# Linear attention in a two-block decoder: state steps issued as one batch, its exponentials moved into the levels, the output product begun on six split tiles

## The chip, the cores and the metric

One Trainium2 chip, of which the kernel uses a single core. Work is done by TensorE (PE in the rows, with its weight load as PEld), VectorE (DVE), ScalarE (ACT) and GpSimd (POOL); SyncE (SP) issues the loads. The metric is the time of the whole kernel on the device in microseconds (us), as a median of runs; a profile is one execution more, taken by the hardware profiler. The granted clock of TensorE is given as a share of 2.4 GHz: 1.00 is that, 0.50 is 1.2 GHz.

## What is computed

Two stacks of two layers on 256 tokens of width 1024, all in float32. The change lies in the first stack, whose layers mix tokens in three ways (a short convolution, an attention with sinks, a gated linear attention) and join them in one product with `w_out`. The first layer works on 512 columns (256 tokens of x, 256 of the context), the second on 256. The part in question, per direction (0 forward, 1 backward) and head:

```python
def step(state, inp):                       # gla_chunk_scan
    b = jnp.cumsum(gc.astype(jnp.float32), axis=2)
    b_last = b[:, :, -1:, :]
    new_state = (jnp.exp(b_last[:, :, 0, :])[..., None] * state
                 + jnp.einsum('bhsk,bhsv->bhkv', kc * jnp.exp(b_last - b), vc))
    ...
    o = (jnp.einsum('bhts,bhsv->bhtv', a, vc)
         + jnp.einsum('bhtk,bhkv->bhtv', qc * jnp.exp(b), state))
    return new_state, o

def gla_output(o, g, norm_g):
    o32 = o32 * lax.rsqrt(jnp.mean(o32 * o32, axis=-1, keepdims=True) + EPS) * norm_g.astype(jnp.float32)
    ...
    return (o32.reshape(B, T, GLA_HEADS * GLA_DV) * jax.nn.silu(g.astype(jnp.float32))).astype(g.dtype)
...
x = x + gt1 * (jnp.concatenate([conv_x, attn_x, gla_x], axis=-1) @ w_out)
```

## The kernel before

Activations lie feature-major: 128 channels of a tile on the partitions, tokens along the free dimension, eight tiles for a width of 1024. Weights come as pieces of 1 MB through `ring`, six slots that SP fills as TensorE frees them. Each large product is made of three in a reduced float format: ScalarE rounds a piece to `ring_hi` (line 220), VectorE takes the remainder `ring_lo` (line 223), and the moving side is split the same way (`a_hi`, and `mix_lo` or `h_lo`). `split_ahead` does this some pieces ahead of TensorE, and `pe_products` runs four output groups side by side over the eight tiles of the input, then the others.

Every engine runs its own program in the order written; engines meet at semaphores, and at `phase_end`, where PE, ACT and DVE wait for one another. In a layer of the first stack the order is: products with `w_in` (`b1_groups`), rope and convolution, attention, gates (`pe_gla_gates`), levels, state steps (`..._gla_out`), head norm (`..._gla_norm`), output product, feed-forward.

**Levels.** The products inside a tile of 128 tokens are built in seven levels. In each, DVE multiplies keys and queries with exponentials (`scaled`, lines 1114 and 1115), takes the differences for the next level (`decay`, lines 1105 and 1106), and copies the masked grams of this level from PSUM (line 1136); ACT takes the exponentials (line 1085); PE makes the grams. Into the six first levels TensorE puts two products of the modulation each (`pe_mod_piece`; ACT copies their rows at line 810). When all levels are done it turns all rows into columns (`pe_mod_columns`) and DVE takes them (`dve_mod_take`).

**State steps.** With four tiles of tokens and two directions there are six steps. For each: ACT takes two exponentials into the single buffer gX (line 1198), DVE multiplies the keys (line 1217), PE turns them (line 1171), ACT copies them (line 1202), PE multiplies them with the values, DVE adds the result to the decayed state (line 1226), and PE uses the state on the next tile's queries. One buffer of each kind serves all steps. The products of grams and values follow.

**Head norm.** ACT copies the sums from PSUM (line 1254), squares them, and for each half of the channels takes a logarithm (line 1260) and an exponential (line 1261) of the head means that PE makes, then Silu of the gate (line 1263). DVE multiplies (lines 1270, 1274). Then the eight tiles of `mixT` are split (lines 473 and 478), then three pieces of `w_out`, then the product starts.

## Time and profile before

| | us |
|---|---|
| median of 3 runs | 2932.71 (2929.97 to 2933.93) |
| the profiled execution, its own time | 2932.67 |
| its span, first to last instruction | 2930.9 |
| TensorE busy | 2595.3 (89%) |
| VectorE busy | 1824.8 (62%) |
| ScalarE busy | 1494.5 (51%) |
| DMA | 561.57 MB, mean 192 GB/s |

The shares are means over stages with different limits. The stages of the change are found by the lines named above in the timeline, once per layer of the first stack: around 288 to 414 us and around 1039 to 1136 us. The rest of the program is not touched in what it does. A row of a timeline gives start, length, engine, line, operation, what is written and read, and in brackets how long the engine had been idle and what ended that. A float32 product counts as two records of TensorE.

### The profile page before, as it was taken

What the parts mean: (1) busy time and instruction counts of PE and PEld (TensorE: products, weight loads), DVE (VectorE), ACT (ScalarE), POOL (GpSimd) and SP (SyncE); (2) the same over time, 40 slices, a digit from 0 to 9 for tenths busy, and PEclk for the clock granted to TensorE, in tenths of its full rate; (3) what the DMA queues carried; (4) which work ended last, traced back from release to release, by engine and by line L of the source; (5) the groups of instructions that cost most, each with busy time, mean ns of one, the idle gap of its engine ahead of it and who ended that gap; (6) DMA issues with size and microseconds to landing.
All of it is one profiled execution on the core that took longest, in us unless ns stands there. A gap on an engine that the chain in (4) does not pass through costs nothing.

```text
span 2930.9 us, 42838 instructions
## 1 busy us (share of the span) xinstructions
PE 2595.3 (89%) x17130; PEld 2294.3 (78%) x17130; DVE 1824.8 (62%) x2532; ACT 1494.5 (51%) x1936; POOL 10.6 (0%) x53
## 2 busy tenths in 40 slices
PE   5987559999999766999878999968799999999997
PEld 3865448999999555998858999948788888888886
DVE  2245736545543554555845554856698889888986
ACT  3225344434442334444455443455577777777775
POOL 0000000000000000000000000000000000000000
PEclk8998869999998866999969999979999999999998
DMA  6241403555532341453404454403299899899994
GB/s 258 99 189 44 173 7 142 182 178 181 187 137 108 115 173 58 173 187 141 162 1 144 144 185 175 159 29 130 85 352 356 337 374 351 338 357 351 354 357 190
DMA packets 80205, 561.57 MB, mean 192 GB/s; under 512 B 8705, under 2 KB 12033, under 8 KB 12434
## 3 DMA queue, kind: packets, MB, share of 16 engines
q1 hardware_dynamic: 79746, 557.86, 51.2%
q8 instruction: 138, 2.26, 0.3%
q0 software_dynamic: 272, 1.05, 0.1%
q14 instruction: 49, 0.40, 0.1%
HBM read 557.82 MB, written 1.05 MB: 191 GB/s over the span
## 4 chain that ended last, share of the span: by engine, by line
PE 52%; DVE 6%; ACT 4%; issue 1%; ACTq 0%; PEldq 0%; DVEq 0%; PEld 0%
PE psum L229 50%; DVE ring_lo L223 2%; DVE Z L1360 1%; ACT ring_hi L220 1%; PE psum L1700 1%; DVE hT L710 1%; PE psum L633 0%; DVE hT L380 0%; ACT L407 0%; DVE xT L313 0%; ACT hT L674 0%; DVE Z L1373 0%; DVE Z L1226 0%; ACTq L183 0%; DVE hT L421 0%
## 5 line engine op out<-in xcount | busy, mean ns | idle before, releaser
L223 DVE TENSOR_TENSOR ring_lo<-ring,ring_hi 128x2048 fp32r<-128x2048 f32 x479 | 1096.5, 2291 | 460.9 <-ACT ring_hi L220 457.9
L220 ACT ACTIVATE ring_hi<-ring 128x2048 fp32r<-128x2048 f32 x479 | 915.9, 1914 | 391.0 <-PE psum L229 389.7
L229 PE MATMUL psum<-a_hi,ring_hi 128*128 128x256 f32 (+1 forms) x2448 | 733.1, 299 | 99.3 <-DVE ring_lo L223 57.4
L229 PE MATMUL psum<-a_hi,ring_lo 128*128 128x256 f32 (+1 forms) x2448 | 729.3, 298 | 0.0
L229 PE MATMUL psum<-h_lo,ring_hi 128*128 128x256 f32 (+1 forms) x2128 | 630.9, 296 | 0.0
L229 PEld LDWEIGHTS psum<-a_hi,ring_hi 128*128 128x128 f32 x2448 | 478.9, 196 | 116.9 <-issue 84.7
L229 PE MATMUL psum<-ring_hi,a_hi 128*128 128x512 f32 (+2 forms) x1744 | 542.5, 377 | 5.9 <-DVE h_lo L429 3.7
L229 PEld LDWEIGHTS psum<-a_hi,ring_lo 128*128 128x128 f32 x2448 | 478.5, 195 | 10.3
L229 PEld LDWEIGHTS psum<-h_lo,ring_hi 128*128 128x128 f32 x2128 | 416.4, 196 | 7.4
L229 PEld LDWEIGHTS psum<-ring_hi,a_hi 128*128 128x128 f32 x1744 | 329.9, 192 | 58.3 <-issue 4.1
L229 PE MATMUL psum<-ring_lo,a_hi 128*128 128x512 f32 (+2 forms) x1040 | 375.1, 361 | 0.0
L229 PE MATMUL psum<-Zr,ring_hi 128*128 128x256 f32 x1408 | 257.3, 286 | 8.1 <-DVE xT L578 8.1
L229 PEld LDWEIGHTS psum<-Zr,ring_hi 128*128 128x128 f32 x1408 | 222.0, 194 | 8.9 <-DVE xT L578 8.9
L229 PEld LDWEIGHTS psum<-ring_lo,a_hi 128*128 128x128 f32 x1040 | 202.0, 194 | 28.2
L229 PE MATMUL psum<-ring_hi,Zr 128*128 128x512 f32 x704 | 219.8, 393 | 0.2
L229 PE MATMUL psum<-Z 64*128 64x128 f32 (+4 forms) x792 | 136.6, 406 | 90.8 <-DVEq L183 28.9
L229 PE MATMUL psum<-Zr,ring_lo 128*128 128x256 f32 x704 | 200.6, 285 | 0.0
L229 PEld LDWEIGHTS psum<-Z 64*128 64x128 f32 (+1 forms) x792 | 86.8, 221 | 124.0 <-issue 36.4
L539 ACT ACTIVATE mixT<-psum 128x256 f32<-128x256 f32 x88 | 33.7, 383 | 262.7 <-PE psum L229 262.7
L229 PEld LDWEIGHTS psum<-ring_hi,Zr 128*128 128x128 f32 x704 | 130.1, 188 | 27.7 <-DVE ring_lo L223 1.8
L229 PE MATMUL psum<-ring_lo,Zr 128*128 128x512 f32 x352 | 137.3, 390 | 0.0
L229 PEld LDWEIGHTS psum<-Zr,ring_lo 128*128 128x128 f32 x704 | 136.5, 194 | 0.0
(249 smaller groups left out, 2515.9 us busy)
## 6 DMA issues: line engine op xcount, KB each, us to landing
ring<-in_stream SPq DMA_DIRECT2D x527, 1024.0 KB, 4.8
cst<-in_constants SPq DMA_DIRECT2D x1, 1216.0 KB
xT<-in_xT SPq DMA_DIRECT2D x1, 1024.0 KB, 9.5
xT<-in_ctxT SPq DMA_DIRECT2D x1, 1024.0 KB, 11.8
xT<-in_memT POOLq DMA_DIRECT2D x1, 1024.0 KB, 6.0
out_y<-hT SPq DMA_DIRECT2D x1, 1024.0 KB, 4.8
Z<-in_level_masks SPq DMA_DIRECT2D x1, 448.0 KB
vec<-in_vectors SPq DMA_DIRECT2D x1, 225.0 KB, 11.0
```

What stands on the lines that cost most here:

```text
L220: e.activation(hi, raw, ACT.Copy).then_inc(sem("piece_rounded"), 1)
L223: e.tensor_tensor(lo, raw, hi.bitcast(F32), ALU.subtract).then_inc(sem("piece_split"), 1)
L229: ins = pe.matmul(*args, **kw)
L539: act.activation(mixT[:, f % 2, 0:T], bank[2 * (f % 2)][:, 0:T], ACT.Silu)\
L710: ins = dve.tensor_tensor_reduce(s_buf(p, i, e)[:, 0:p["nk"]], src, p["mask"], 1.0, p["init"][e], ALU.add, ALU.max, cols(i, MAX)[:, e:e + 1])
L1360: ins = dve.scalar_tensor_tensor(z2(6 + c), CP[:, c, j:j + T], w, z2(6 + c), ALU.mult, ALU.add)
L1700: ins = pe.transpose(bank[2 + j % 2][:, c * P:(c + 1) * P], hid_tok[j % 2][:, c * P:(c + 1) * P], const("ident"))
```

## The change

- **Exponentials.** Those of the queries (`gQ`, one of 1024 or 512 columns a direction) stand behind levels 3 and 4 of ACT's program, those of the keys (six of 128 columns a direction, into six buffers `gK`) behind levels 4 and 5, and tiles 0 to 5 of `mixT` are rounded behind levels 0 to 2. DVE multiplies the keys in three instructions in the last level, ahead of its masked copies, and the queries behind them.
- **Modulation columns.** Each level turns the rows of the level before, four products at a time; the second layer turns the four pieces of the rope stage ahead of its levels. The rows lie in tiles 6 and 7 of `mixT`.
- **State steps.** All six turns, copies (three, two steps each) and key products are independent of the states, go to PSUM banks 4 to 6 and are issued as a batch with the products of grams and values between them. ACT copies the first state of each direction; DVE makes the other four with full 128x128 tiles. States have six buffers. ACT rounds two pieces of `w_out` ahead of its copies, and DVE takes their remainders between the state steps.
- **Head norm and output product.** ACT reads the sums from PSUM. Both logarithms, then both exponentials. Silu of the gate is taken when the gate leaves PSUM in `b1_groups`. The output product is issued behind the last use of a state, with the head means behind its first tile; tiles 6 and 7 are split last. It uses banks 2, 3, 4 and 7.
- Three phase ends a layer are gone from ACT, DVE and PE (levels, state steps, head norm; none is left between gates and the end of the layer's output product).

```diff
-        def pe_products(pe, groups, ready, who=None, late=None):
+        def pe_products(pe, groups, ready, who=None, late=None, at=range(4), inside=lambda k: None):
...
                     if g == front - 1:
+                        inside(k)
                         await_next(pe, ready)
...
-            g += feature_major([zt(15), zt(16)], 0, n)
+            for out, (terms, rows_, width, _, held) in zip((zt(15), zt(16)), feature_major([None, None], 0, n)):
+                g.append((terms, rows_, width, [("function", out, ACT.Silu)], held))
             g += feature_major([lrT(0), lrT(1)], 0, 2 * T, rows_=16)
             return g
 
+
+        B1_WHO = [("act", "dve")[g % 2] for g in range(22)] + ["dve", "act", "act", "dve", "act"]
...
+        KEY_TILES = ((0, 2, 3), (1, 2, 3))
+        STEPS = ((0, 2), (0, 3), (1, 3), (1, 2), (1, 1), (0, 0))
...
+            if layer:
+                pe_mod_columns(pe, IN_ROPE[1])
...
+                if l and in_level(layer, l - 1):
+                    pe_mod_columns(pe, in_level(layer, l - 1))
                 for m in in_level(layer, l):
                     pe_mod_piece(pe, m)
-            first, end = batch(layer)
-            pe_mod_columns(pe, first, end - first, rows_a)
...
-            phase_end(pe)
+            pe.wait_ge(sem("gram_read"), base(pe, "gram_read"))
...
                 for m in in_level(layer, l - 1) if l else ():
-                    act_mod_rows(act, m, batch(layer)[0], rows_a)
-            for m in in_level(layer, LEVELS - 1):
-                act_mod_rows(act, m, batch(layer)[0], rows_a)
-            phase_end(act)
+                    act_mod_rows(act, m)
+                if l < 3:
+                    if layer and l == 0:
+                        act.wait_ge(sem("mod_columns"), ROPE_COLUMNS)
+                    act_split_mix(act, (2 * l, 2 * l + 1), n)
+                if l in (3, 4):
+                    d = l - 3
+                    act.activation(gQ[:, d, :, 0:n], gB[d][:, :, 0:n], ACT.Exp).then_inc(sem("query_exp"), 1)
+                if l in (4, 5):
+                    d = l - 4
+                    for i, t in enumerate(KEY_TILES[d]):
+                        edge = t * P + (P - 1 if d == 0 else 0)
+                        for c in range(2):
+                            ins = act.activation(gK[:, d, c, i, :], gB[d][:, c, t * P:(t + 1) * P], ACT.Exp, scale=-1.0,
+                                                 bias=gB[d][:, c, edge:edge + 1])
+                    ins.then_inc(sem("key_exp"), 1)
...
+                else:
+                    await_next(dve, "key_exp", 2)
+                    for out, t0, t1 in ((gK[:, 0, :, 1:3, :], 2, 4), (gK[:, 1, :, :, :], 1, 4), (gK[:, 0, :, 0:1, :], 0, 1)):
+                        k = GK[:, :, t0 * P:t1 * P].rearrange("p c (s n) -> p c s n", n=P)
+                        dve.tensor_tensor(out, out, k, ALU.mult).then_inc(sem("keys_decayed"), 1)
...
+            await_next(dve, "query_exp", 2)
+            for d in range(2):
+                dve.tensor_tensor(gQ[:, d, :, 0:n], gQ[:, d, :, 0:n], GQ[:, :, 0:n], ALU.mult)\
+                   .then_inc(sem("queries_decayed"), 1)
...
+        def state(d, i):
+            return 3 * d + i
+
+        def kv(j):
+            return bank[4 + j // 2][:, (j % 2) * 256:(j % 2 + 1) * 256]
...
+            def turn(b):
+                await_next(pe, "keys_decayed")
...
+                for j in (2 * b, 2 * b + 1):
+                    d, t = STEPS[j]
+                    for c in range(2):
+                        ins = pe.transpose(kv(j)[:, c * P:(c + 1) * P], gK[:, d, c, KEY_TILES[d].index(t), :],
+                                           const("ident"))
+                ins.then_inc(sem("keys_turned"), 1)
...
+            def within(ts):
+                for t in ts:
+                    for h in range(4):
+                        mm(pe, gO[(h % 2) * HD:(h % 2 + 1) * HD, h // 2, t, :],
+                           tok[:, t * 384 + P + h * HD:t * 384 + P + (h + 1) * HD], gA[:, t, h, :],
+                           start=t % 2 == 0 and h < 2, stop=False, skip_group_check=True)
...
+            def step(b):
+                await_next(pe, "keys_copied")
+                for j in (2 * b, 2 * b + 1):
+                    t = STEPS[j][1]
+                    for c in range(2):
+                        mm(pe, kv(j)[:, c * P:(c + 1) * P], gKt[:, j, c * P:(c + 1) * P],
+                           tok[:, t * 384 + P + c * P:t * 384 + P + (c + 1) * P], start=True, stop=True,
+                           last_of="state_step" if j % 2 and c == 1 else None)
...
+            turn(0)
+            turn(1)
+            within(outs[0:2])
+            turn(2)
+            step(0)
+            step(1)
+            within(outs[2:])
+            step(2)
+            await_next(pe, "queries_decayed", 2)
+            first = base(pe, "state_first")
+            own = base(pe, "state")
+            uses = [(i, d) for i in range(3) for d in range(2) if ORDER[d][i + 1] in outs]
...
+            for i, d in uses:
+                t = ORDER[d][i + 1]
+                if i == 0:
+                    pe.wait_ge(sem("state_first"), first + d + 1)
+                else:
+                    pe.wait_ge(sem("state"), own + 2 * (i - 1) + d + 1)
+                for c in range(2):
+                    for r in range(2):
+                        rr = slice(r * HD, (r + 1) * HD)
+                        last = (i, d) == uses[-1] and c == 1 and r == 1
+                        mm(pe, gO[rr, c, t, :], gS[rr, state(d, i), c, rr], gQ[rr, d, c, t * P:(t + 1) * P],
+                           start=False, stop=True, skip_group_check=True, last_of="gla_sum" if last else None)
...
+        def act_gla_out(act, layer):
+            split_ahead(act, "act", 0)
+            for b in range(3):
+                await_next(act, "keys_turned")
+                act.activation(gKt[:, 2 * b:2 * b + 2, :].rearrange("p j n -> p (j n)"), bank[4 + b][:, :], ACT.Copy)\
+                   .then_inc(sem("keys_copied"), 1)
...
+                await_next(act, "state_step")
+                act.activation(gS[:, state(d, 0), :, :].rearrange("p c n -> p (c n)"), kv(2 * d), ACT.Copy)\
+                   .then_inc(sem("state_first"), 1)
+            advance(act, "state_step", 1)
...
+            def step(d, i):
+                t = ORDER[d][i]
+                j = STEPS.index((d, t))
+                for c in range(2):
+                    ins = dve.scalar_tensor_tensor(gS[:, state(d, i), c, :], gS[:, state(d, i - 1), c, :],
+                                                   gD[:, d, t, c:c + 1], kv(j)[:, c * P:(c + 1) * P], ALU.mult, ALU.add)
+                link(dve, ins)
+                dve.nop().then_inc(sem("state"), 1)
...
+            dve_split_mix(dve, (0, 1), n)
+            split_ahead(dve, "dve", -1)
             for d in range(2):
...
+                await_next(dve, "state_step")
+                await_next(dve, "state_first")
+                step(d, 1)
+            split_ahead(dve, "dve", 1)
+            await_next(dve, "state_step")
             for d in range(2):
...
+                step(d, 2)
+            dve_split_mix(dve, range(2, 6), n)
...
+            n = 2 * T if layer == 0 else T
+            act.preload_act_table_set("natural_log")
+            await_next(act, "gla_sum")
...
             for c in range(2):
-                act.activation(gSq[:, c, 0:n], o[:, c, :], ACT.Square).then_inc(sem("gla_squared"), 1)
+                act.activation(by_tile(gSq[:, c, :], n), gO[:, c, 0:n // P, :], ACT.Square).then_inc(sem("gla_squared"), 1)
...
             for c in range(2):
                 await_next(act, "gla_mean_square")
-                link(act, act.activation(gR[:, c, 0:n], bank[4 + c][:, 0:n], ACT.Ln, bias=EPS))
+                ins = act.activation(gR[:, c, 0:n], bank[5 + c][:, 0:n], ACT.Ln, bias=EPS)
+            link(act, ins)
+            for c in range(2):
...
+                await_next(act, "gla_normed")
+                act_split_mix(act, (6 + c,), n)
```

TensorE, first layer, from the last level on. In the order views x2 counts like instructions in a row; before, this stands six times in a row (three are shown), followed by the sixteen products within tiles and the two head means:

```order
L1171 MATMUL psum<-cst,Z 128x128 x2
L229 MATMUL psum<-tok,Z 128x128 x2
L229 MATMUL psum<-Z 128x128 x2
L1171 MATMUL psum<-cst,Z 128x128 x2
L229 MATMUL psum<-tok,Z 128x128 x2
L229 MATMUL psum<-Z 128x128 x2
```

and now, once, ending in the first product of the output (`cst,mixT` are the last columns, `cst,Z` turns, `Z,tok` products within tiles, `tok,Z` key products, `hT,Z` uses of the states):

```order
L229 MATMUL psum<-cst,mixT 128x2 x4
L1201 MATMUL psum<-cst,Z 128x128 x8
L229 MATMUL psum<-Z,tok 64x128 x8
L1201 MATMUL psum<-cst,Z 128x128 x4
L229 MATMUL psum<-tok,Z 128x128 x8
L229 MATMUL psum<-Z,tok 64x128 x8
L229 MATMUL psum<-tok,Z 128x128 x4
L229 MATMUL psum<-hT,Z 64x128 x24
L229 MATMUL psum<-a_hi,ring_hi 128x512
```

The turns no longer alternate with key products and uses, and the output product has moved ahead of the head means.

ScalarE, first layer, before: the head norm up to the weight pieces.

```order
L1260 ACT_TABLE_LOAD
L1260 ACTIVATE hT<-psum 128x512
L1261 ACT_TABLE_LOAD
L1261 ACTIVATE hT<-hT 128x512
L1260 ACT_TABLE_LOAD
L1260 ACTIVATE hT<-psum 128x512
L1261 ACT_TABLE_LOAD
L1261 ACTIVATE hT<-hT 128x512
L1263 ACT_TABLE_LOAD
L1263 ACTIVATE hT<-Z 128x512 x2
L473 ACTIVATE a_hi<-mixT 128x512 x8
L220 ACTIVATE ring_hi<-ring 128x2048 x3
```

and now, from the weight pieces on:

```order
L220 ACTIVATE ring_hi<-ring 128x2048 x2
L1252 ACTIVATE Z<-psum 128x512 x3
L1256 ACTIVATE Z<-psum 128x256 x2
L1301 ACT_TABLE_LOAD
L1304 ACTIVATE hT<-psum 128x512 x2
L1307 ACTIVATE hT<-psum 128x512 x2
L1310 ACT_TABLE_LOAD
L1310 ACTIVATE hT<-hT 128x512 x2
L474 ACTIVATE a_hi<-mixT 128x512 x2
L220 ACTIVATE ring_hi<-ring 128x2048
```

Two pieces went ahead of the state steps, six of the eight tiles into the levels, and two table loads stand where five stood. Two others are new in each layer: one ahead of Silu in `b1_groups`, one ahead of the attention's first exponential.

## Rows read from the trace of the kernel before

**Rows 1.** The page, part 2: granted clock of TensorE in 40 equal slices.
```profile
PEclk8998869999998866999969999979999999999998
```
**Rows 2.** Busy time by stretch, first layer (columns: stretch, length, engines, clock, DMA, GB/s).
```profile
287.60:342.10 54.50, 33.76 (x449) 24.32 (x449) 53.27 (x91) 19.41 (x26) 0.00 (x0) 0.91 0.58 213
342.10:349.20 7.10, 7.05 (x50) 6.96 (x48) 1.11 (x3) 0.00 (x0) 0.00 (x0) 0.76 0.36 144
349.20:389.40 40.20, 21.32 (x92) 16.26 (x92) 12.95 (x42) 9.07 (x34) 0.00 (x0) 0.50 0.00 1
389.40:403.40 14.00, 1.95 (x4) 0.68 (x4) 2.80 (x4) 12.69 (x17) 0.00 (x0) 0.74 0.00 0
403.40:414.30 10.90, 0.01 (x1) 0.04 (x1) 9.66 (x11) 10.84 (x12) 0.00 (x0) 0.50 0.00 0
414.30:462.30 48.00, 48.00 (x198) 38.04 (x198) 18.63 (x25) 10.35 (x12) 0.00 (x0) 0.97 0.19 69
```
**Rows 3.** The same view, second layer.
```profile
1039.00:1069.70 30.70, 24.08 (x320) 15.36 (x320) 28.71 (x73) 13.17 (x27) 0.00 (x0) 0.84 0.66 263
1069.70:1081.40 11.70, 11.04 (x66) 10.95 (x64) 1.47 (x4) 0.00 (x0) 0.00 (x0) 0.63 0.94 390
1081.40:1115.20 33.80, 17.69 (x68) 12.64 (x68) 11.09 (x35) 7.48 (x26) 0.00 (x0) 0.50 0.00 0
1135.50:1163.50 28.00, 27.18 (x198) 26.49 (x198) 13.91 (x17) 8.62 (x12) 0.00 (x0) 0.90 0.30 114
```
**Rows 4.** Timeline, first layer: one state step, then the products within tiles.
```profile
361.51 0.63 PE L1171 MATMUL psum<-cst,Z 128*128 128x128 f32 x2
...
362.62 1.22 PE L229 MATMUL psum<-tok,Z 128*128 128x128 f32 x4 [0.47 <-ACT Z L1202]
363.88 1.16 DVE L1226 SCALAR_TENSOR_TENSOR Z<-Z,sc,psum 64x64 f32<-64x64 f32 x4 [2.92 <-PE psum L229]
...
385.70 3.68 PE L229 MATMUL psum<-Z,tok 128*64 128x128 f32 x32
```
**Rows 5.** Timeline, first layer: head means and the first logarithm of the head norm.
```profile
391.91 1.95 PE L229 MATMUL psum<-hT,cst 128*128 128x512 f32 x4 [2.53 <-ACT hT L1257]
...
392.30 1.28 ACT L1260 ACT_TABLE_LOAD   x1
...
393.60 0.60 ACT L1260 ACTIVATE hT<-psum 128x512 f32<-128x512 f32 x1
```
**Rows 6.** Timeline, first layer: weight remainders, then two of the first output products.
```profile
409.54 6.70 DVE L223 TENSOR_TENSOR ring_lo<-ring,ring_hi 128x2048 fp32r<-128x2048 f32 x3 [0.44 <-ACT ring_hi L220]
...
414.85 0.63 PE L229 MATMUL psum<-mix_lo,ring_hi 128*128 128x512 f32 x1
...
415.27 0.63 PE L229 MATMUL psum<-a_hi,ring_lo 128*128 128x512 f32 x1
```
**Rows 7.** Timelines of TensorE, VectorE and ScalarE: from levels of both layers.
```profile
1043.35 2.08 PE L229 MATMUL psum<-Z 64*128 64x128 f32 x16 [2.19 <-DVE Z L1115]
...
1061.62 1.93 PE L229 MATMUL psum<-ring,c_mat 128*32 128x256 f32 x32
1064.58 1.16 PE L229 MATMUL psum<-Z 64*128 64x128 f32 x16 [1.03 <-DVE Z L1115]
...
340.64 2.55 DVE L1136 COPY_PREDICATED Z<-lvl_mask,psum 128x512 f32<-128x512 uint8 x4 [0.87 <-DVE Z L1115]
...
333.74 2.26 ACT L1085 ACTIVATE Z<-Z 128x1024 f32<-128x1024 f32 x2 [2.50 <-DVE Z L1106]
...
1061.30 1.30 ACT L1085 ACTIVATE Z<-Z 128x512 f32<-128x512 f32 x2 [1.34 <-DVE Z L1106]
...
1104.68 0.68 ACT L1198 ACTIVATE Z<-hT 128x128 f32<-128x128 f32 x2
```
**Rows 8.** Busy time by stretch: two microseconds within the modulation columns.
```profile
1071.00:1073.00 2.00, 2.00 (x19) 2.00 (x19) 0.00 (x0) 0.00 (x0) 0.00 (x0) 0.95 1.05 434
```
**Rows 9.** Timeline, first layer: the first exponential of the attention.
```profile
206.36 0.72 ACT L674 ACTIVATE hT<-hT,sc 128x513 f32<-128x513 f32 x1 [9.41 <-DVE sc L718]
```

221 lines of the change are left out of this document (74 added, 147 removed).

## The prediction

> **What bounds the kernel now.** I began with the granted clock over the span [rows 1]: it is full in most of the span and falls in two early places. They are the stages of the change. Busy time by stretch tells who is late in each. In the levels of the first layer VectorE works 53.27 of 54.50 us: it is the bound. Behind them nobody is: TensorE makes columns for 7.10 us (VectorE idle), the state steps and inner products take 40.20 us with every engine busy half the time or less and the clock at 0.50, the head norm 14.00 us on ScalarE, and the splits before the product 10.90 us with TensorE still [rows 2]. Those are 72.2 us from the last level to the first output product, at 414.3. The second layer repeats it: 11.70 us of columns, 33.80 us of steps, and the product starts at 1135.5 [rows 3], 65.8 us after 1069.7. From 414.3 to 462.3 TensorE is busy all the time [rows 2]; nothing before the product can hide behind it while it waits for all eight tiles. So 138 us in the two layers are chains of waits, and DMA idles in them with a full ring: these are not transfer limits. The timeline shows the chain of one step: turn 0.63 us, copy, key product 1.22, state on VectorE 1.16, then the use [rows 4]; six of them run one after another through single buffers.
>
> **Levels, what is added.** First layer. Columns cost 2 us for 19 records at a clock of 0.95 [rows 8]; all 64 of the second layer took 11.04 us at 0.63 on the mean [rows 3]. So two pieces (8 records) cost 0.84 us of TensorE a level, or 1.4 at that mean. Its work by level there leaves room: 33.76 busy of 54.50 us [rows 2]. ScalarE gets six rounded tiles, two wide exponentials and twelve narrow ones. It is busy 19.41 of 54.50 us; between exponentials it waits 2.50 us each level [rows 7]. Behind level 4 stand one wide exponential (half the pair's 2.26 us) and six narrow ones at about 0.3 each (0.68 the pair) [rows 7], 2.9 us in all; with the rows now later by 0.84 that puts the next level 0.3 us late. VectorE's product of the keys is 1536 columns. A two-source float32 pass costs 6.70 / 3 = 2.23 us for 2048 columns [rows 6], 1.09 ns a column: 1.7 us, of which 0.87 fall where it waits today ahead of the last masked copies [rows 7]. So the last masked copy ends 1.3 us later, at about 344.5.
>
> Second layer. A level lasts about 4.05 us, of which TensorE is idle 1.03 [rows 7]. Adding 0.84 leaves 0.2, so it stays hidden at full clock. At half clock, where this stage begins, the four rope pieces (16 records) cost 2.8 us or more, of which 2.19 were idle [rows 7]: 0.7 us late. ScalarE idles 1.34 us a level [rows 7] but gets 2.5 us behind level 4 and 1.9 behind level 5, besides later rows: 1.5 us of stall. With the keys' 1.2 the last copy ends 3.4 us later, at 1074.2. Bounds for this whole term: 1.5 (everything but the keys hidden) to 6 us.
>
> **State steps as a batch.** Two queues decide, and I cost both from the last masked copy on.
> VectorE, first layer: queries 2048 columns 2.2 us, taking the columns 0.9, two tiles split 1.1, one weight piece 2.2, two states 1.4, a second piece 2.2, two states 1.4: 11.4. (A state is two instructions; the old four of 64x64 took 1.16, so 0.29 each [rows 4], and 0.1 to close.) Then one use: 344.5 + 11.4 + 0.7 = 356.6 at the earliest.
> TensorE at half clock: 12 turns, 0.63 for two: 3.8; 12 key products, 1.22 for two with the start of the pipe, 0.85 without: 5.1 to 7.3; inner products 3.68 [rows 4]; 24 uses on quarter tiles like the inner products, 0.23 each: 5.5. Together 18.1 to 20.3, so 362.6 to 364.8. At full clock half of it, and VectorE decides. I take 360: the engine comes from full clock, and such mixed work as the old steps ran at 0.50 but with half of the time idle. The output product then starts 414.3 - 360 = 54.3 us earlier (49.5 to 57.7).
> Second layer: VectorE 1.1 + 0.5 + 0.6 + 2.2 + 1.4 + 2.2 + 1.4 = 9.4; TensorE at half 3.8 + 5.1 + 1.8 + 3.7 = 14.4 to 16.6. From 1074.2: 1084.1 to 1090.8; I take 1087. Gain 48.5 us (44.7 to 51.4).
> ScalarE rounds two pieces before it copies the turned keys, 3.8 us. They must have landed: in the second layer DMA is still at 390 GB/s behind the levels [rows 3], and 1 MB takes 2.7 us. I have the second piece down by about 1073 and the rounding done by 1075, with the turns: no wait, or 2 us if it lands late. Behind the weight pieces VectorE now holds the states: one that is ready waits up to 2.2 us for a remainder on VectorE, counted above.
>
> **Head norm and first splits.** They leave the path if TensorE has enough to do. In the first layer slow products follow each other every 0.42 us [rows 6]; the 48.00 us hold 192 of them and a few others, some of the first slow, so a fast one takes some 0.23 [rows 2]. The first tile is 12 products, tiles 1 to 5 are 60: 13.7 us. From the head means to the last split I count two logarithms 1.2, a load 1.28, exponentials 0.6 to 1.2, four passes of VectorE 2.4, a rounded tile and a remainder 1.2, links 0.6: 7 to 8 us. Hidden. In the second layer 28.00 us for as many products [rows 3] is the half: 60 of them 7.1 us fast, against a chain of 5.6. Hidden by 1.5 us only; uncovered in full it would cost 5.6 and 7 to 8 us. The means themselves stay on TensorE between tiles: 1.95 us for two [rows 5] at the lower clock, so 1.5 in the first and 1.0 in the second layer is paid.
> The table load shows as 1.28 us, with the next instruction 0.02 us behind it [rows 5]. The Trainium skill, ScalarE: Activation LUTs, section "What ACT_TABLE_LOAD costs", has a drain of some 1.38 us besides, 2.66 in all. The trace disagrees with that here; by the page the second layer's norm would no longer be hidden and the time would be about 1 us longer, and each load that is added below 1.4 dearer.
>
> **Silu moved.** Its copy from PSUM replaces a copy; its load falls where ScalarE is idle. The load before the attention stands behind the wait for the first maxima, which today releases the exponential at 206.36 after 9.41 us of idle time [rows 9]: it can't use that idle time. Exposed: 0 to 1.3 us a layer. VectorE has the next pair to reduce meanwhile; I take 0.5 for the first layer and 0 for the second.
>
> **The sum**, against the profiled execution's own 2932.67 us: 54.3 - 1.5 - 0.5 = 52.3 in the first layer, 48.5 - 1.0 = 47.5 in the second, 99.8 in all. 2832.9, so 2833. The profiled execution is within 0.1 of the median of the runs. After the product everything is as before: it is TensorE's, and the loads have more slack than they use.
>
> **Bounds.** Both layers bound by VectorE: 57.7 + 51.4 - 2.5 = 106.6, and if the clock is already full when the output product starts, its slow beginning (0.42 against 0.23) also goes, some 4 us: 2822. Both at TensorE's slow end with a late weight piece and 1.3 us per layer for the attention: 49.5 + 44.7 - 2.5 - 2.6 - 2 = 87: 2846.
>
> **The rivals.**
> 1. The head norm isn't hidden. For: the cover of the second layer is 7.1 us against 5.6, and each semaphore has its delay. Against: at half clock the cover doubles. TensorE waits at tile 6 for 2 to 5 us a layer: 2837 to 2843, inside the range.
> 2. The clock falls in the levels. For: over the 11.70 us of columns it was 0.63 on the mean, and 0.76 over the 7.10 of the first layer, though the engine was busy throughout [rows 2, 3], and now columns stand in each level. Against: they come in runs of 0.84 us between products that held 0.91 and 0.84 over the whole levels. The levels would turn to TensorE's: in the second layer 2.08 of grams, 1.4 of columns and twice 1.93 of modulation [rows 7], 7.3 instead of 4.05 over six levels, 19 us, and some 6 in the first layer: 2858.
> The Trainium skill, TensorE: Matmul & The Clock Gate, Part 1, ties the clock to how busy the engine has been lately. By it alone neither the columns nor the batch would lose the clock, and rival 3 would follow; the row above speaks against it.
> 3. VectorE alone bounds the batch, at full clock: 2822 to 2826, as in the bounds.
> 4. It doesn't do what it says: a wait joins the batch to the chain after all (a buffer still shared, a key product behind a state). For: banks 4 to 6 hold turns and products in turn. Against: in the order no wait for a state stands ahead of the uses. Then half of the 40 and 34 us comes back, and the time is near 2868.
> 5. Slower than before. TensorE enters the output product at half clock and stays there into the feed-forward that follows. A product costs 0.42 instead of 0.23, so each us of full-rate work costs 0.83 us more; 100 us are eaten after 120 us of such work, and 300 us of it would end near 3080. Against: after each of today's starts from 0.50 the clock was back within 6 us of streaming [rows 3, 6].
>
> **Chances.** Forecast, within the bounds 2822 to 2846: 0.70; rival 1: 0.09; rival 2: 0.07; rival 3: 0.08; rival 4: 0.04; rival 5: 0.02. To hold 8 in 10 the range takes in the forecast's bounds, rival 1 and the near part of rivals 2 and 3: 2820 to 2850. Faster by over 0.2% (5.9 us, about what a measurement of this kernel can tell from no change) is every case but the last: 0.97; 0.01 for no change, 0.02 for slower.
>
> **What would show it.** First output product near 360 us and near 1087, behind a batch in which no key product waits for a state; columns in runs of eight records inside the levels; the last masked copy about 1 and 3 us later than now; no idle of TensorE at tiles 6 and 7; 192 products at the same pace. Wrong: a gap of TensorE before the head means or tile 6, levels of the second layer much over 4.1 us, ScalarE waiting for a weight piece with turned keys ready, or a clock of 0.50 beyond the first six us of a product.

## The result, and the profile after

| kernel | median, us | lowest to highest | executions |
|---|---|---|---|
| before | 2931.34 | 2928.34 to 2933.93 | 4 |
| after | 2816.58 | 2812.88 to 2821.54 | 4 |

The ratio is 0.962 (95% interval 0.959 to 0.965). In a second series it was 0.961 (0.958 to 0.964), with a median of 2812.61. By the medians the kernel is 114.8 us faster, where I had forecast 99.7 and a range of 2820 to 2850. The profiled execution of after took 2812.88 us (span 2810.6), 119.8 less than that of before.

Busy time by stretch, kernel after: levels, batch and output product of the first layer, then of the second. They answer to [rows 2] and [rows 3]; the columns are stretch, length, busy time and number of records of PE, PEld, DVE, ACT and POOL, granted clock, DMA share, GB/s.

```profile
287.70:344.25 56.55, 42.76 (x496) 31.83 (x496) 56.19 (x96) 30.91 (x48) 0.00 (x0) 0.83 0.57 209
344.25:357.07 12.82, 10.46 (x116) 9.02 (x116) 11.85 (x20) 3.76 (x7) 0.00 (x0) 0.93 0.16 66
357.07:406.17 49.10, 49.05 (x204) 38.29 (x202) 24.53 (x34) 19.32 (x23) 0.00 (x0) 0.98 0.19 68
974.07:1008.04 33.97, 31.07 (x384) 22.97 (x384) 31.72 (x78) 20.81 (x48) 0.00 (x0) 0.90 0.69 279
1008.04:1018.97 10.93, 8.47 (x84) 7.03 (x84) 10.04 (x19) 5.42 (x7) 0.00 (x0) 0.93 0.70 291
1018.97:1046.70 27.73, 26.49 (x204) 25.61 (x202) 17.25 (x25) 16.24 (x23) 0.00 (x0) 0.97 0.34 118
```

The 71.1 us from the end of the last masked copy to the first output product (72.2 by the marks of [rows 2]) have become 12.8, and VectorE, which worked 12.95 of 40.20 us in the old steps, is busy 11.85 of 12.82 here. TensorE runs near the full clock (0.93 on the mean), not at 0.50. Who is late at the end of the batch is seen on the timeline of VectorE and then of TensorE, kernel after, first layer:

```profile
344.15 2.35 DVE L1177 TENSOR_TENSOR hT<-hT,Z 128x1024 f32<-128x1024 f32 x2
...
347.28 1.29 DVE L479 TENSOR_TENSOR mix_lo<-mixT,a_hi 128x512 fp32r<-128x512 f32 x2
348.49 2.28 DVE L223 TENSOR_TENSOR ring_lo<-ring,ring_hi 128x2048 fp32r<-128x2048 f32 x1
350.69 0.60 DVE L1268 SCALAR_TENSOR_TENSOR Z<-Z,sc,psum 128x128 f32<-128x128 f32 x2
...
352.25 2.29 DVE L223 TENSOR_TENSOR ring_lo<-ring,ring_hi 128x2048 fp32r<-128x2048 f32 x1
354.46 1.35 DVE L1268 SCALAR_TENSOR_TENSOR Z<-Z,sc,psum 128x128 f32<-128x128 f32 x4
```
```profile
346.86 1.95 PE L229 MATMUL psum<-tok,Z 128*128 128x128 f32 x16
...
350.85 2.03 PE L229 MATMUL psum<-hT,Z 64*64 64x128 f32 x32
355.17 1.97 PE L229 MATMUL psum<-hT,Z 64*64 64x128 f32 x16 [2.30 <-DVEq L1271]
357.07 0.79 PE L229 MATMUL psum<-a_hi,ring_hi 128*128 128x512 f32 x1
```

VectorE goes through its list with hardly a pause (11.85 of 12.82 us busy): queries, two tiles, a weight remainder, two states, the other remainder, two states. TensorE has used all earlier states by 352.9 and waits 2.30 us for the last two. In the second layer the same wait is 2.28 us. So VectorE's list sets the start of the product in both layers; TensorE's own work in the batch adds up to 11.0 us and would have let it start some 1.7 us earlier (an estimate from these rows: 344.31, where its first turn begins, and 11.0).

**Where the 119.8 us lie.** Between marks that both programs have (loads of ScalarE's tables):

| stretch | before | after | gained | predicted |
|---|---|---|---|---|
| layer 0, end of the gates to the norm after the product | 179.11 | 122.87 | 56.2 | 52.8 |
| layer 1, the same | 128.69 | 76.12 | 52.6 | 47.5 |
| layer 1, w_in products to gates | 165.15 | 156.50 | 8.7 | 0 |
| everything else | | | 2.3 | -0.5 |

The second profiles of both kernels give 59.5 and 52.0 us for the first two lines, so these gains are known to some 3 us. The third stretch runs from the norm ahead of layer 1's w_in products through its attention to the gates; the change touches in it only Silu, with its table, and which engine empties the last w_in groups from PSUM. Busy time by stretch there, kernel before (three stretches), then kernel after (one):

```profile
896.00:902.00 6.00, 4.49 (x23) 3.51 (x22) 4.14 (x4) 4.29 (x5) 0.00 (x0) 1.00 0.41 167
902.00:926.00 24.00, 24.00 (x115) 24.00 (x115) 3.71 (x4) 2.67 (x4) 0.00 (x0) 0.50 0.13 44
926.00:932.00 6.00, 6.00 (x40) 5.51 (x40) 1.15 (x3) 2.21 (x2) 0.00 (x0) 1.00 0.20 53
```
```profile
848.00:872.00 24.00, 24.00 (x171) 22.41 (x170) 6.19 (x6) 4.63 (x5) 0.00 (x0) 1.00 0.24 89
```

Before, TensorE made 115 products in 24 us at a clock of 0.50, busy all the time; after, 171 at 1.00. Whether that belongs to the change was the first question.

### The profile page after: what moved, and what is told of

Its sections match the earlier page's. It is cut to its first block, busy times and chain, and to the rows that moved or that the text cites. A ratio compares the mean times of both kernels' runs of the same rounds, so it can differ in the third digit from the quotient of the medians.

```text
span 2810.6 us, 42790 instructions
## 1 busy us (share of the span) xinstructions
PE 2556.6 (91%) x17170; PEld 2262.9 (81%) x17170; DVE 1813.2 (65%) x2484; ACT 1484.5 (53%) x1902; POOL 10.7 (0%) x53
## 4 chain that ended last, share of the span: by engine, by line
PE 79%; DVE 11%; ACT 5%; issue 2%; DMA 1%; SPq 0%; ACTq 0%; PEldq 0%; DVEq 0%; POOL 0%
PE psum L229 78%; DVE ring_lo L223 3%; ACT ring_hi L220 1%; PE psum L634 1%; DVE Z L1411 1%; DVE hT L711 1%; DMA ring<-in_stream 1%; PE psum L1751 1%; ACT hT L675 1%; DVE hT L422 1%; DVE Z L1171 1%; ACT L408 0%; DVE Z L1145 0%; DVE hT L381 0%; DVE Z L1144 0%
## 5 line engine op out<-in xcount | busy, mean ns | idle before, releaser
L229 PE MATMUL psum<-Z 64*128 64x128 f32 (+3 forms) x752 | 124.7, 404 | 66.3 <-DVEq L183 28.2
L229 PEld LDWEIGHTS psum<-Z 64*128 64x128 f32 (+1 forms) x752 | 77.7, 216 | 96.9 <-issue 35.9
## 6 DMA issues: line engine op xcount, KB each, us to landing
xT<-in_ctxT SPq DMA_DIRECT2D x1, 1024.0 KB, 12.1
```

The costliest lines, as they stand in the source:

```text
L229: ins = pe.matmul(*args, **kw)
```

## The experiments

My theories: **V**, VectorE's list bounds the batch, against **T**, TensorE bounds it as in my sum. **G**, a gap of TensorE in the w_in products lets the clock fall there, against **C** or **N**, it falls by itself, and **S**, each schedule (the order of work in a kernel) has its own places. All profiles in one table, in us: from the table load at the end of the gates to the last masked copy, from there to the first output product, and the whole to the norm after the product; then the segment of layer 1's w_in products, and the times.

| kernel | layer 0 | layer 1 | w_in | median (range) |
|---|---|---|---|---|
| before | 59.3, 71.1, 179.1 | 35.4, 64.7, 128.7 | 165.2 | 2931.3 (2928.3 to 2933.9) |
| before_again | 59.4, 73.0, 181.0 | 36.0, 65.2, 129.3 | 165.1 | 2931.3 (2914.6 to 2934.6) |
| before_filled | 59.3, 70.0, 178.9 | 35.6, 64.4, 127.4 | 155.0 | 2916.0 (2914.0 to 2922.7) |
| after | 60.4, 12.8, 122.9 | 37.4, 10.9, 76.1 | 156.5 | 2816.6 (2812.9 to 2821.5) |
| after_again | 60.2, 12.3, 121.5 | 38.5, 11.1, 77.2 | 165.9 | 2812.6 (2807.3 to 2821.3) |
| wait_filled | 64.1, 12.7, 126.7 | 38.8, 10.8, 77.5 | 155.0 | 2810.0 (2806.1 to 2817.7) |
| wait_all_tiles | 64.1, 24.2, 137.4 | 37.4, 18.4, 83.9 | 156.4 | 2842.1 (2833.8 to 2843.3) |
| states_first | 60.2, 12.8, 124.5 | 37.5, 12.7, 78.7 | 155.8 | 2820.5 (2813.6 to 2827.9) |
| product_by_piece | 64.1, 10.1, 123.1 | 38.8, 8.2, 73.9 | 155.0 | 2803.4 (2799.7 to 2813.9) |
| silu_after_norm | 60.9, 12.3, 123.7 | 38.6, 10.8, 77.2 | 166.2 | 2819.5 (2809.7 to 2823.5) |
| columns_three_times | 67.6, 12.3, 128.9 | 53.1, 13.9, 94.5 | 166.1 | 2847.9 (2836.8 to 2850.7) |
| steps_chained | 60.3, 19.9, 129.1 | 38.6, 16.7, 82.2 | 166.1 | 2835.8 (2831.6 to 2837.6) |
| by_piece_and_filled | 60.4, 10.1, 119.4 | 37.4, 8.2, 72.6 | 156.5 | 2800.4 (2799.2 to 2806.9) |

**Both kernels once more.**

> The kernel before, unchanged, profiled a second time. In its first profile the w_in products of layer 1 ran at a clock of 0.50 from 902 to 925 us although TensorE was busy throughout, and that is where 8.6 us of the difference between the two profiles lie. If that stretch belongs to this kernel's schedule (theory S), the second profile shows it again between 900 and 926 us, and the layer-1 table load of the attention ends up within 1 us of the first. If the clock falls there by chance (theory C), the second profile can have the stretch at 1.00 and be some 8 us shorter there, with other stretches at 0.50 elsewhere; the time stays within 2925 to 2940.

> The kernel after, unchanged, profiled a second time and timed in more rounds. Its four times so far lie in two pairs, 2812.9 and 2813.4, 2819.8 and 2821.5. Theory C (stretches at half clock come and go from execution to execution): times between 2811 and 2823 again with gaps of some 7 us between groups, and a second profile whose offsets differ from the first by a few us in a stage that the change does not touch, with the granted clock at 0.50 there. Theory S (the change moved later stages for good): the offsets of all stages within 1 us of the first profile, and the stretch of layer 1's w_in products at 1.00. The stages of the change themselves: 56 and 53 us shorter than before by either.

Before again had the stretch, so S alone looked right; but after again had it too, and the first profile of after had not. Busy time by stretch, second profile of after:

```profile
839.00:845.00 6.00, 4.49 (x24) 3.54 (x23) 4.46 (x4) 4.18 (x4) 0.00 (x0) 0.98 0.37 154
845.00:869.00 24.00, 24.00 (x115) 24.00 (x115) 3.64 (x4) 2.47 (x3) 0.00 (x0) 0.51 0.13 44
```

The two profiles of the kernel after are of the same program, so the 8.7 us are no fixed effect of the change: the kernel after can have the stretch or not. The kernel before has it in both of its profiles; that it can do without is read from its times only, five of seventeen of which lie some 15 us under the others. S falls.

**What lets the clock fall.** Six products ahead of TensorE's wait for the late tile, once in the kernel after, once in the kernel before:

```
+                    if late == 10 and g == late and k == len(group[0]) - 1:
+                        terms, _, n, _, _ = groups[g]
+                        for _ in range(6):
+                            mm(pe, bank[5][:, 0:n], terms[0][0](weights[g][0], 0), terms[0][1](weights[g][0], 0),
+                               start=True, stop=True)
                     if late and g == late:
                         await_next(pe, "late_split")
```

> The kernel after with six more products of 512 columns into an unused bank just before TensorE's wait for the late split tile in layer 1's w_in products, a wait of 1.51 us (842.8 in the second profile of the kernel after). Nothing is left out; their results are not used. In three of six profiles so far the clock fell to 0.50 from 1.6 us behind that wait and stayed there some 23 us, which made this segment (table load of the FFN's norm to that of the gates) 165 instead of 156 us. Theory G (this gap of TensorE lets the clock fall): the segment is 156 us in the profile, plus at most 0.3, and the times lose their upper group: median 2807 to 2813, spread below that of the kernel after. Theory N (the gap has nothing to do with it, the clock falls by itself in about half of the executions): times in the same two groups, and even chances for the 165 us.

> The kernel before with the six filling products (results not used) ahead of TensorE's wait for the late split tile in layer 1's w_in products; nothing else is changed. In both profiles of the kernel before the clock fell to 0.50 right behind that wait and stayed there for 23 to 24 us (segment of 165.1 us, 156 without it), and its times lie in two groups: most at 2928 to 2939, about one in four at 2913 to 2918. Theory G (that gap of TensorE is where the clock is lost): the segment is 155 to 156 us and the times go to the lower group, 2914 to 2924, 10 us or more faster than the kernel before. Theory N (the clock falls by itself): the same two groups with the same shares, median 2931, ratio within 0.2%.

Timeline of TensorE: kernel before, then before_filled, and its busy time behind the wait:

```profile
900.61 0.50 PE L229 MATMUL psum<-a_hi,ring_hi 128*128 128x512 f32 x1 [1.51 <-DVE h_lo L431]
...
901.69 0.27 PE L229 MATMUL psum<-ring_hi,a_hi 128*128 128x128 f32 x1
...
902.34 0.41 PE L229 MATMUL psum<-ring_lo,a_hi 128*128 128x128 f32 x1
```
```profile
898.65 1.52 PE L229 MATMUL psum<-a_hi,ring_hi 128*128 128x512 f32 x6
900.34 0.51 PE L229 MATMUL psum<-a_hi,ring_hi 128*128 128x512 f32 x1 [0.17 <-DVE h_lo L436]
```
```profile
902.00:926.00 24.00, 24.00 (x175) 22.58 (x175) 7.01 (x7) 4.68 (x5) 0.00 (x0) 1.00 0.22 89
```

With 0.17 us of waiting left instead of 1.51 the clock stays, and the segment is 155.0. The median of the kernel before falls by 15.4 us, 0.4% (ratio 0.9964, 0.9946 to 0.9981), by six products whose results nobody uses. All its twelve times lie below 2923; of the kernel before, measured beside it, twelve of seventeen lie between 2928 and 2938 and five below 2921. G holds in so far as the clock is lost behind this gap and kept when it is filled. The gap alone doesn't decide: of ten profiles without the filling products six had the stretch, of three with them none, and all ten had the same wait of 1.50 to 1.52 us. Nor do the runs tell the shorter wait from the six wide products themselves; six such products beside an unshortened wait weren't tried. In the kernel after the gain is smaller: its median was 2812.6 and 2816.6 in two series, 2810.0 with the gap filled, and the ranges overlap.

**How much the overlap with the product is worth.** The product waits for all eight tiles, with the head means ahead of it:

```
+                pe_head_means(pe, layer)
+                pe.wait_ge(sem("mix_split"), base(pe, "mix_split") + KT)
+                pe_products(pe, out_groups(KT, n, gate_gain(layer, 0), 2), "mix_split", "dve", at=OUT_BANKS)
```

> The kernel after, but the output product of both linear attentions waits for all eight split tiles as before; the head means come ahead of it. Nothing is left out. By my terms this uncovers what six tiles hid: in the first layer from the squares at 357.2 to the last split at 369.4 is 12.2 us, of which 1.9 were paid as head means, in the second 1019.1 to 1027.2, 8.1 of which 1.3: together 17 us, and some 4 us more if TensorE then begins the product at half clock: slower than the kernel after by 17 to 21 us, 2833 to 2838. If the overlap were worth less, because TensorE is late anyway (rival: TensorE bounds the stage), 5 to 10 us, below 2827.

Timeline of TensorE, first layer:

```profile
361.33 3.78 PE L229 MATMUL psum<-hT,cst 128*128 128x512 f32 x4 [0.70 <-ACT hT L1304]
372.03 0.79 PE L229 MATMUL psum<-a_hi,ring_hi 128*128 128x512 f32 x1 [6.91 <-DVE mix_lo L479]
...
373.05 0.63 PE L229 MATMUL psum<-a_hi,ring_lo 128*128 128x512 f32 x1
```

TensorE waits 6.91 us and comes back slow (0.43 us a product). Product starts 11.6 and 7.4 us later, 19 in the two layers, against 17 expected: that is what beginning the product on six tiles is worth. The median is 25 to 29 us up, at 2842 instead of 2833 to 2838: the overlap (19), the slow beginning, and in the profile 3.8 us in the layer 0 levels (below). What the rest is was not found.

**VectorE's list.** First both remainders behind all states:

```
-            split_ahead(dve, "dve", -1)
             for d in range(2):
                 await_next(dve, "state_step")
                 await_next(dve, "state_first")
                 step(d, 1)
-            split_ahead(dve, "dve", 1)
             await_next(dve, "state_step")
             for d in range(2):
                 step(d, 2)
+            split_ahead(dve, "dve", -1)
+            split_ahead(dve, "dve", 1)
```

> The kernel after, with VectorE's two remainders of weight pieces behind all four states instead of one ahead of each pair. Nothing is left out. Theory V (VectorE's passes alone bound the batch, at full clock; TensorE waited 2.30 us for the last states in layer 0): the last states come 4.4 us earlier less a wait of about 0.8 for the first, so the output product starts 3 us earlier in each layer, and the remainders are late for its third and seventh product by less than 1.5 us: 2 to 6 us faster in all. Theory T (TensorE bounds the batch, as I had it in the sum): no change in the start of the product, and the remainders then cost 1 to 2 us a layer: 1 to 4 us slower.

Timeline of VectorE, then of TensorE:

```profile
353.37 1.36 DVE L1268 SCALAR_TENSOR_TENSOR Z<-Z,sc,psum 128x128 f32<-128x128 f32 x4 [1.02 <-PE psum L229]
354.87 4.49 DVE L223 TENSOR_TENSOR ring_lo<-ring,ring_hi 128x2048 fp32r<-128x2048 f32 x2
```
```profile
359.47 0.76 PE L229 MATMUL psum<-a_hi,ring_hi 128*128 128x512 f32 x1 [3.37 <-DVE ring_lo L223]
...
360.45 0.63 PE L229 MATMUL psum<-a_hi,ring_lo 128*128 128x512 f32 x1
```

A miss, and neither theory is decided by it: I had overlooked that TensorE waits for both weight pieces before its first product. The start stayed at copy + 12.8 and moved to + 12.7 in the second layer. Whatever the order of the list, its end sets the start; and the wait of 3.37 us now stands right before the product, which begins at half clock. So the remainder was moved and the wait with it: the first two tiles of the product are made for the first piece's two groups before TensorE waits for the second piece, whose remainder alone goes behind the states.

```
+                if inside and g == 2:
+                    for k in range(2):
+                        await_next(pe, ready)
+                        for first in range(2):
+                            term(first, k)
+                    inside(1)
                 weights.append(piece_slot(pe) if group[4] == "new" else weights[-1])
...
-            split_ahead(dve, "dve", 1)
             await_next(dve, "state_step")
             for d in range(2):
                 step(d, 2)
+            split_ahead(dve, "dve", 1)
```

> The kernel after with two changes: VectorE's second remainder of a weight piece goes behind all states, and TensorE makes the first two tiles of the output product for the two groups of the first piece (12 products) before it waits for the second piece. Nothing is left out. In the run with both remainders behind the states, TensorE had the last state used 3.4 us earlier but began the product at the same distance from the last masked copy (12.8 us), because it waits for both remainders before its first product. Theory V (VectorE's list of passes sets the start of the product, at full clock): the product starts 2.2 us earlier, at last masked copy + 10.5 us in the first layer, with no wait for the second remainder beyond 1 us: each of the two stages 1.5 to 2.5 us shorter than 122 and 76.5, 3 to 5 us in all, near 2809. Theory T (TensorE sets it): no change, within 1 us.

Timeline of VectorE and TensorE, second layer:

```profile
1014.29 2.11 DVE L1275 SCALAR_TENSOR_TENSOR Z<-Z,sc,psum 128x128 f32<-128x128 f32 x6 [0.21 <-DVE Z L1275]
1016.54 2.29 DVE L223 TENSOR_TENSOR ring_lo<-ring,ring_hi 128x2048 fp32r<-128x2048 f32 x1
```
```profile
1017.09 0.39 PE L229 MATMUL psum<-a_hi,ring_hi 128*128 128x256 f32 x1
...
1018.62 1.02 PE L229 MATMUL psum<-hT,cst 128*128 128x256 f32 x4
```

The product starts 2.2 to 2.9 us earlier in each layer, about the length of one remainder (2.29), at full clock. V holds, T falls. The same change uses up most of what VectorE held back: in the first layer's batch TensorE is now busy 9.80 of 10.05 us and VectorE 9.07. The median is 2803.4, 9 to 13 us under the kernel after, where I had expected 3 to 5; the two stages account for 4.5 to 7 of them (leaving out the layer 0 levels), the rest was not located.

**Independence of the steps.** TensorE waits for a state before it turns the next pair of keys (and ScalarE copies the first states between the keys):

```
+            own = base(pe, "state")
             turn(0)
+            within(outs[0:2])
+            step(0)
+            pe.wait_ge(sem("state"), own + 1)
             turn(1)
...
+            pe.wait_ge(sem("state"), own + 2)
             turn(2)
```

> The kernel after, but the state steps' pairs run one after another: TensorE turns the second pair of keys only when the first state of the first pair is there, and the third pair only when the next is. Nothing is left out. It measures what independence within the batch is worth, apart from the wide instructions and the exponentials in the levels. In the kernel after the output product starts 12.3 to 12.8 us behind the last masked copy in the first layer and 10.8 to 11.1 in the second. Each of the two added waits puts turn, copy, key product and copy of a pair (1.1 + 0.6 + 1.0 + 0.4, with 0.3 of links: 3.4 us at full clock) behind a state, while VectorE does a weight remainder of 2.3 in one of them: 5 to 7 us a layer, start at 18 to 19 us and 16 to 18, and TensorE, idle more than half of the time, would go to half clock, 2 us more a layer: 2825 to 2833. If VectorE's list alone counted (pure theory V) and the chain fitted beside it: less than 2 us a layer.

Busy time by stretch, from the last masked copy to the first output product, both layers:

```profile
343.97:363.83 19.86, 15.60 (x116) 13.22 (x116) 12.86 (x21) 3.84 (x6) 0.00 (x0) 0.66 0.09 35
1025.34:1042.05 16.71, 11.61 (x84) 9.71 (x84) 10.41 (x20) 4.75 (x7) 0.00 (x0) 0.69 0.43 177
```

7.3 and 5.7 us more, where I had expected 5 to 7, and here part of the clock is gone: 0.66 and 0.69. (TensorE isn't idle more than half of the time, as I had written, but busy 15.60 of 19.86 us.) Even chained, three wide pairs take 19.9 us with the products within tiles and two weight remainders, where the six narrow steps took 40.2 us with the products within tiles [rows 2]. This run prices the independence of the steps. How the rest divides between the wide tiles, the exponentials in the levels and the columns in the levels was not measured.

**Silu behind the norm again.**

```
...
+            for c in range(2):
+                act.activation(hflat[:, 2048 + c * 512:2048 + c * 512 + n], Zt[:, 15 + c, 0:n], ACT.Silu)\
+                   .then_inc(sem("gla_silu"), 1)
...
```

> The kernel after with Silu of the gates back in the head norm, behind the two exponentials; the w_in products copy the gates plainly again. Nothing is left out. My terms: the table load before layer 0's attention goes (0.5 us gained, the first profile showed 0.7), the norm chain grows by a table load of 1.28 and two Silus of 0.6 or 0.4, 2.4 and 2.1 us. In the first layer six tiles hide it (last split at 371.8 against some 373 for tile 6), in the second the cover was used to within 1.5 us: TensorE waits some 1 us there. Stages: layer 0 within 0.3 us of 122.2 (mean of two profiles), layer 1 0.5 to 1.5 us over 76.7; in all 0 to 1 us slower than the kernel after, which the times can't tell. Rival: the norm isn't hidden in either layer already now, then each stage is 2 us longer.

Timeline of ScalarE, second layer:

```profile
1037.53 1.28 ACT L1311 ACT_TABLE_LOAD   x1
1038.83 0.72 ACT L1311 ACTIVATE hT<-Z 128x256 f32<-128x256 f32 x2
```

ScalarE's part is 2.0 us longer in the second layer, but the last split comes only 1.1 us later after the start of the product (9.4 us against 8.2), and TensorE doesn't wait in either product. In the kernel after the last split ends at 1027.20 and TensorE reaches tile 6 at 1029.34: a cover of 2.1 us, of which 1.0 is left here. In the first layer the split comes 1.9 us later, also hidden. The stages (123.7, 77.2) are 0.9 to 2.2 and 0 to 1.1 us over those of the two profiles of the kernel after, which differ by 1.4 and 1.1 themselves; the ranges of the times overlap. So a price of Silu's place can't be told from these runs.

**Columns three times.**

```
...
-                    pe_mod_columns(pe, in_level(layer, l - 1))
+                    pe_mod_columns(pe, in_level(layer, l - 1), 3)
```

> The kernel after, but the columns of the modulation inside the levels are made three times in a row (24 records a level instead of 8, the last ones count). Nothing is left out. Eight records take 1.05 us at full clock here. Layer 0: TensorE was busy two thirds of the levels, VectorE sets their pace, and there are 3 or more us a level of idle TensorE; two more sets of 1.05 us in five levels and behind the last: hidden but for at most 2 us, stage 122 to 124. Layer 1: a level has 0.2 us of slack left by my sum, so 2.1 us more a level come out at about 1.9 each over five levels and in full behind the last: 9 to 12 us longer, stage 86 to 89. Rival (the clock falls under columns, as it did in the 11.70 us block of the kernel before at 0.63): the levels run at 0.50 and the stages become 10 and 20 us longer.

Busy time by stretch in layer 1's levels of this run:

```profile
1011.50:1017.50 6.00, 6.00 (x62) 3.74 (x62) 2.95 (x8) 2.32 (x5) 0.00 (x0) 0.72 0.75 285
1017.50:1023.50 6.00, 6.00 (x51) 3.78 (x52) 2.41 (x7) 0.93 (x3) 0.00 (x0) 0.56 0.72 251
1023.50:1029.50 6.00, 6.00 (x62) 4.92 (x64) 4.26 (x10) 3.52 (x10) 0.00 (x0) 0.78 0.88 343
```

The result lies between my sum and the rival, nearer to the rival in layer 1: its levels took 15 us more, where the added columns at full clock come to 9 to 12, because TensorE, busy 6.00 of 6.00 us, had only 0.56 to 0.78 of its clock for much of the time. Layer 0's levels took 7 us more, not 2 at most.

The same happens in a small way in the kernel after, in layer 0. The kernel before, then the kernel after, at the same place:

```profile
308.00:314.00 6.00, 2.80 (x44) 2.07 (x36) 5.96 (x11) 2.69 (x4) 0.00 (x0) 1.00 0.95 370
```
```profile
308.00:314.00 6.00, 5.34 (x64) 3.32 (x65) 5.96 (x10) 2.95 (x6) 0.00 (x0) 0.77 0.49 175
```

From 302 us to the last level the kernel before holds 1.00 in its three profiles until the columns behind the levels begin; every profile of the kernel after and its variants loses part of the clock there: its lowest value over six us lies between 0.50 and 0.79. VectorE sets the pace of these levels (5.96 of 6.00 us busy in both rows), so this mostly stays hidden. My rival 2 was thus a real mechanism, which the kernel after doesn't avoid: it costs it little here, not the 6 us in this layer that I had named.

**The best of it.**

> The faster variant of the batch (second remainder behind the states, the product begun on the first weight piece) together with the six filling products ahead of the late wait in layer 1. Nothing is left out. The first alone had a median of 2803.4 (2799.7 to 2813.9), the second 2810.0 (2806.1 to 2817.7) against 2812.6 to 2816.6 of the kernel after. Theory G: the upper group disappears, 2799 to 2805, median near 2801. Theory N: median within 2 us of 2803.4 and again a value above 2810. Product starts at last masked copy + 10.0 and + 8.2 us by either.

2800.4 us, ratio 0.957 (0.954 to 0.959): faster than both kernels, 131 us under the kernel before. The profile has the shortest stages of all, 119.4 and 72.6, and no stretch at half clock in the w_in products.

**One thing stays open.** Nine profiles have the levels of the kernel after. In layer 0 six of them need 60.2 to 60.9 us to the last masked copy, three others 64.1, with the same instructions; in those three the clock was lost more than once and late in the levels, so that VectorE, which else sets the pace, had to wait (1.49 us for a product of TensorE at the last level). Busy time by stretch, wait_filled:

```profile
338.00:344.00 6.00, 5.88 (x44) 4.10 (x48) 5.86 (x10) 0.91 (x2) 0.00 (x0) 0.50 0.31 127
```

The kernel before held 1.00 here until its columns began. No run says what decides it, and none has these levels without the columns. It is worth 3.8 us in an execution that has it.

## Why the prediction was wrong, point by point

1. **Levels.** Right in the first layer: last masked copy at 344.25 (344.5 predicted). In the second it came 37.4 us after the gates, 1072.8 on the time axis of the kernel before, where I had 1074.2 (38.5 us, or 1073.9, in the second profile): ScalarE's stall behind level 4 was 1.24 us, and little else showed.
2. **The batch: the step that failed.** "TensorE at half clock: ... I take 360". I took the clock of the old steps (0.50) for work that no longer waits. TensorE did its 12 turns in 1.75 us, the key products in 3.1, the inner products in 2.2 and the uses in 4.0: 11.0 us at nearly full clock, against my 18.1 to 20.3. VectorE decided, as in rival 3, to which I had given 0.08. My list for VectorE was nearly right: 12.1 us from the last copy in the first layer (12.3 to 12.8 measured), 9.9 in the second (10.9 to 11.1). The start came at 357.07 and at 1083.7 on the old axis, not 360 and 1087: 2.9 and 3.3 us, of which 1.4 in the second layer are the levels of point 1. The chained run, at 0.66 and 0.69, shows that the doubt had a ground. By the Trainium skill, TensorE: Matmul & The Clock Gate, Part 1, activity releases the throttle. In the batch the trace agrees: 0.93, where the waiting steps had 0.50. In the w_in products it doesn't: 24.00 of 24.00 us busy at 0.50.
3. **Slow beginning of the product.** I left it out of the sum and charged the head means. It went in part: in the second layer start to norm took 27.75 us with the head means in it, against 28.52 before, 1.8 us better than my sum; in the first 49.70 against 48.67, 0.5 us better.
4. **Head norm.** Hidden, as predicted; the cover in the second layer was 2.1 us, near my 1.5, so rival 1 was not far off.
5. **Silu.** 0.5 us predicted for the first layer; the gates end 0.05 us apart in the two kernels. That is less than the profiles of one kernel differ there, so the term is neither confirmed nor refuted.
6. **"After the product everything is as before": the other step that failed.** The granted clock [rows 1] shows an 8 in the slice from 879 to 952 us, and a 6 and a 7 further back, besides the two early places that I named; I took all the rest as fixed. In the first of them lay 8.7 us of the difference between the profiles, and 2.3 us were spread over everything else. By times the share is known less well, since both kernels can lose the clock there: with the gap filled in both, 2916.0 against 2810.0 in two series, the change is worth 106.0 us. That is near my bound for "both layers bound by VectorE", 106.6; the sum said 99.8. That the other 9 of the 114.8 are the stretch is inferred from this difference, not measured by itself.

So the chain of waits went away as predicted, and two terms were off. The stages gained 8.5 us more than my sum: some 4.5 by the clock of the batch, 1.7 by earlier last copies, 2.2 by the product's quicker beginning. That alone would have given about 2824, inside the range; the stretch outside the change, which I had put at nothing, and which the first profile of the kernel after happened not to have, carried the result past its end.

## What to carry to other kernels

When a chain of waits becomes a batch, don't carry the granted clock of the chain's rows over to the new work: add it up at both clocks, and beside it the whole list of the next engine, which may become the bound. Read the granted clock over the whole span before summing, because a stretch at half clock outside the change can come or go between two kernels, and even between two executions of one; compare stages between marks, not only medians. And where TensorE waits a microsecond or two before a long row of small products, try a few useless products in the gap and measure: they paid 15.4 us in the kernel before, and nothing that can be told from the spread in the kernel after.

## What the runs showed of the hardware that I had not expected

- Behind a wait of 1.51 us the clock fell to 0.50 in six of ten profiles and stayed there while TensorE was busy without a pause with products of 128 columns. In the kernel before it rose again at 926, while products of 256 columns ran, which had begun at 921. With the same wait the stretch ran at 1.00 in the other four, one of them a profile of the very program that had 0.51 in another.
- The stretch costs 10.2 us in its segment (165.2 against 155.0), and the medians of the kernel before differ by 15.4 us. Where the other 5 lie isn't shown: the profiles with and without the stretch also differ by 1 to 2 us in places ahead of it.
- A TensorE that is busy 6.00 of 6.00 us can run at 0.56 to 0.78 of its clock where products with two moving columns stand between the others (24 records a level); with 8 records a level it had 0.77 over six us at 308 in layer 0, where the kernel before, without them, had 1.00.
